# Last attention of a two-block model on one Trainium2 core: TensorE's scores issued for two steps at a time

## The chip, the cores and the metric

One core of one Trainium2 chip runs the whole program in one launch. The metric is the device time in microseconds (us), as the median of several runs. Engines are called TensorE (PE in the profile, PEld for its weight loads), VectorE (DVE), ScalarE (ACT), GpSimd (POOL) and SyncE (SP).

## The reference

The program computes two model blocks in a row on 512 tokens of width 1024. The first has a gated linear recurrence layer and a gated linear attention layer. The second has feed-forward layers, a stick-breaking attention and, last, an attention with three branches, whose mixer is what this document is about (16 query heads of 64, 4 key/value groups):

```python
s_c = einsum('btgrd,bcgd->bgrtc', q, k_c) * scale          # 31 compressed keys
p_c = softmax(where(valid_c, s_c, NEG)) * any(valid_c)
o_c = einsum('bgrtc,bcgd->btgrd', p_c, v_c)
o_s = _nsa_selected(q, sel_idx, k_s, v_s)                  # selected blocks
o_w = _nsa_window(q, k_w, v_w)                             # window of 512
o = gates[0] * o_c + gates[1] * o_s + gates[2] * o_w
return o.reshape(B, S, H * Dh) @ w_out
```

With 512 tokens there are 8 key blocks of 64 and 8 are selected, so the selected branch, like the window branch, is causal attention over all keys. One more feed-forward layer follows.

## The kernel before, in words

Each engine has one hand-written stream of instructions; the streams meet only by semaphores (`wait_ge` before an instruction, `then_inc` after it), and each engine takes its stream in order. Weights stream through a ring of four slots: SyncE loads a slot when GpSimd has split the one before it, GpSimd splits a weight into a high and a low part (L332, L334), and TensorE multiplies with three products per tile (L364 to L366).

The last attention (TensorE L1186 to L1281, ScalarE L1640 to L1677, VectorE L2260 to L2345, GpSimd L2419 to L2437) runs over 8 pairs of heads and six kinds of step per pair, 48 steps in all (`NSA_STEPS`, L574). `nsa_step(s)` gives pair s // 6, kind s % 6 and PSUM slot s % 2 * 2. Kinds 0 to 4 hold parts of the causal score matrix (`NSA_PARTS`, L572): kinds 0 and 2 have one part of 512 keys, kinds 1 and 3 have two parts (128 and 384 keys), kind 4 has two of 256. Kind 5 is the compressed branch. Each part exists for two heads. A step s passes through these operations:

- TensorE, scores (`nsa_scores`, L1186): products of queries and keys into the PSUM banks of slot s % 2, then the mask products (L1213, L1202). It waits for `probs_ready` of step s - 2 (L1194), which last read that slot.
- VectorE, maxima (`nsa_maxima`, L2260): the row maxima out of PSUM (L2279) and the bias; for kind 5 three passes (L2267, L2271, L2274).
- ScalarE, exponentials (`nsa_probs`, L1640): one activation per part and head (L1652), each with a read of the accumulated sum, and at the end `probs_ready`; one activation (L1645) for kind 5. From step 4 on it waits for the transposes of step s - 4.
- VectorE, coefficients (`nsa_coef`, L2292): gate over sum (L2311, L2313).
- GpSimd, scaling (`nsa_scale`, L2419): the probabilities times the coefficients (L2430; L2424 for kind 5).
- TensorE, transposes (`nsa_turn`, L1217): eight 128x128 transposes into PSUM banks 4 and 5 (L1231; L1229 for kind 5). They wait for the scaling of the step and for both copies of step s - 1.
- Copies of the transposed halves out of PSUM: bank 4 by VectorE (`nsa_low_half`, L2318), bank 5 by ScalarE (`nsa_high_half`, L1660).
- TensorE, values (`nsa_attend`, L1234): products with the values (L1253; L1245 for kind 5). They wait for both copies of step s.

After the last kind of a pair, ScalarE and VectorE read the pair's result (`nsa_mix_high` L1664, `nsa_mix_low` L2322). The output projection (`out_pe`) and the last feed-forward layer follow.

The order of each stream is written out by hand. In iteration `it` of its loop (L1275) TensorE issues the scores of step it + 2, the transposes of it - 1 and the values of it - 2. ScalarE (L1671) issues the copy of it - 1, the exponentials of it + 2, and, once a pair, the mix copy. VectorE (L2332) issues the maxima of it + 2, the coefficients of it + 1, the copy of it - 1, and, once a pair, the low mix; where step it + 2 is of kind 5 the copy and the coefficients come ahead of the maxima. In iterations 1 to 6 VectorE also carries the rotation of the last query tile (L2228, L2233, L2239, L2241).

Of the kernel before, what the change touches and what calls it, by code (L numbers as in the profile page):

```python
# [104 lines left out]
def build(nc, x_in, consts_in, gates_in, weights, out):  # L105
    ctx = ExitStack()
    with ctx:
# [72 lines left out]
        for name, slots, cols in STREAM:  # L180
            first[name] = n0
            n0 += slots
        slots_of = {name: slots for name, slots, _ in STREAM}
        cols_of = {name: cols for name, _, cols in STREAM}

        def used(name, n):
# [207 lines left out]
        def out_pe(pe, name, x_hi, x_lo, lows, free, banks=(4, 5, 6, 7)):  # L394

            def low_ready(k):
                return pe.wait_ge(sem["mix_low"], lows + k + 1)

            pe.wait_ge(sem["w_ready"], ready(name, 1))
            product(ps[:, banks[0], :], 0, DT, x_hi, x_lo, low_ready, last_k=DT - 1)  # L400
            pe.wait_ge(sem["w_ready"], ready(name, 2))
            product(ps[:, banks[1], :], 1, DT, x_hi, x_lo, last_k=3)
            product(ps[:, banks[0], :], 0, DT, x_hi, x_lo, low_ready, first_k=DT - 1)
            product(ps[:, banks[1], :], 1, DT, x_hi, x_lo, first_k=3)
            for m in range(2, DT):
                if m >= RING:
                    pe.wait_ge(sem[free[0]], free[1] + m - RING + 1)
                pe.wait_ge(sem["w_ready"], ready(name, m + 1))
                product(ps[:, banks[m % RING], :], m, DT, x_hi, x_lo)
# [153 lines left out]
        def pr_of(s, e):  # L563

            return prt[:, 1, e, :] if s == 0 else (root, acc)[e] if s == 1 else pr[:, s % 4, e, :]
# [8 lines left out]
        NSA_STEPS = SB_PAIRS * NSA_KINDS  # L574

        def nsa_step(s):

            return s // NSA_KINDS, s % NSA_KINDS, s % 2 * 2
# [51 lines left out]
        def _(pe):  # L630
# [520 lines left out]
            def q_norms(m):  # L1151
                pe.wait_ge(sem["q_copied"], m + 1)
                if m == 4:
                    pe.wait_ge(sem["norms_read"], 1)
                for t in range(TT):
                    mm = nc.tensor.matmul(ps[:, 7, t * 16 + 2 * m:t * 16 + 2 * m + 2], sq_q[:, m % 2, t * P:(t + 1) * P],
                                          con("halves")[:, 0:P:64], start=True, stop=True)
                mm.then_inc(sem["norms_mm"], 1)
# [27 lines left out]
            def nsa_scores(s):  # L1186

                p, kind, slot = nsa_step(s)
                if kind == 0:
                    pe.wait_ge(sem["q_rotated"], p + 1)  # L1190
                if s == 0:
                    pe.wait_ge(sem["q_shifted"], 6)
                if s >= 2:
                    pe.wait_ge(sem["probs_ready"], s - 1)  # L1194
                if kind == NSA_KINDS - 1:
                    for t in range(TT):
                        for e in range(2):
                            rows = slice(64 * e, 64 * e + 64)
                            nc.tensor.matmul(ps[:, slot + e, t * N_CMP:(t + 1) * N_CMP], q_r[rows, p, t * P:(t + 1) * P],
                                             k_c3[rows, p // 2, :], start=(t == 0), stop=False, skip_group_check=True)  # L1200
                    for e in range(2):
                        mm = nc.tensor.matmul(ps[:, slot + e, 0:TT * N_CMP], ident_1, neg_c_1, start=False, stop=True,  # L1202
                                              skip_group_check=True)
                else:
                    for i, (br, t, at) in enumerate(NSA_PARTS[kind]):
                        for e in range(2):
                            rows = slice(64 * e, 64 * e + 64)
                            nc.tensor.matmul(ps[:, slot + e, at:at + (t + 1) * P], q_r[rows, p, t * P:(t + 1) * P],
                                             k_sw[rows, p // 2 + 4 * br, 0:(t + 1) * P], start=(i == 0), stop=False,
                                             skip_group_check=True)  # L1210
                    for br, t, at in NSA_PARTS[kind]:
                        for e in range(2):
                            mm = nc.tensor.matmul(ps[:, slot + e, at + t * P:at + (t + 1) * P], ident_1, causal_1,  # L1213
                                                  start=False, stop=True, skip_group_check=True)
                mm.then_inc(sem["z2_done"], 1)

            def nsa_turn(s):  # L1217

                p, kind, _ = nsa_step(s)
                pe.wait_ge(sem["scaled"], s + 1)  # L1220
                if s == 0:
                    pe.wait_ge(sem["q_shifted"], 7)
                if s > 0:
                    pe.wait_ge(sem["low_half"], s)
                    pe.wait_ge(sem["high_half"], s)
                for e in range(2):
                    for t in range(TT):
                        if kind == NSA_KINDS - 1:
                            mm = nc.tensor.transpose(ps[0:N_CMP, 4 + e, t * P:(t + 1) * P], pr_c[:, e, t, :], ident)  # L1229
                        else:  # L1230
                            mm = nc.tensor.transpose(ps[:, 4 + e, t * P:(t + 1) * P], pr_of(s, e)[:, t * P:(t + 1) * P], ident)  # L1231
                mm.then_inc(sem["turned"], 1)

            def nsa_attend(s):  # L1234

                p, kind, _ = nsa_step(s)
                pe.wait_ge(sem["low_half"], s + 1)
                pe.wait_ge(sem["high_half"], s + 1)
                if kind == 0 and p == 1:
                    pe.wait_ge(sem["norms_read"], 2)  # L1240
                if kind == 0 and p >= 2:
                    pe.wait_ge(sem["mix_low"], 2 * DT + p - 1)
                if kind == NSA_KINDS - 1:
                    for e in range(2):
                        mm = nc.tensor.matmul(ps[64 * e:64 * e + 64, 6 + p % 2, :], v_c3[0:N_CMP, p // 2, :],  # L1245
                                              prt[0:N_CMP, s % 2, e, :], start=False, stop=True, skip_group_check=True)
                    mm.then_inc(sem["attended"], 1)
                    return
                first_mm = kind == 0
                for br, t, at in NSA_PARTS[kind]:  # L1250
                    for t2 in range(t + 1):
                        for e in range(2):
                            nc.tensor.matmul(ps[64 * e:64 * e + 64, 6 + p % 2, t * P:(t + 1) * P],  # L1253
                                             v_sw4[:, t2, p // 2 + 4 * br, :],
                                             prt[:, s % 2, e, at + t2 * P:at + (t2 + 1) * P],
                                             start=first_mm, stop=False, skip_group_check=True)
                        first_mm = False
# [14 lines left out]
            q_norms(DT - 2)  # L1272
            nsa_scores(2)
            q_norms(DT - 1)
            for it in range(1, NSA_STEPS + 2):  # L1275
                if it + 2 < NSA_STEPS:
                    nsa_scores(it + 2)
                if it - 1 < NSA_STEPS:
                    nsa_turn(it - 1)
                if 0 <= it - 2:  # L1280
                    nsa_attend(it - 2)  # L1281
            out_pe(pe, "nsa_out", mix2_hi, mix2_lo, 2 * DT, ("res_done", RES["nsa_out"]))
            ffn_pe("ffn2", 1, 3)

# [1075 lines left out]
        def _(pool):  # L2360
# [23 lines left out]
            for j in range(1, 2 * RING):  # L2384
                split_slot(pool, "odd_out", j // RING, j % RING)
            split_first(pool, "ffn1_in_0_0")
            split_pool(pool, *(name for name, _, _ in ffn_stream("ffn1", 0)[1:]), "sb_qk", "sb_v", "sb_late",
                       "sb_out", *(name for name, _, _ in ffn_stream("ffn2", 0)), "kv_c", "kv_kv")
            for n in range(7):
                split_slot(pool, "cmp_w1", n // RING, n % RING)  # L2390
# [214 lines left out]
```

## Time and profile before

| | us |
|---|---|
| median of 3 runs | 2743.24 (2742.39 to 2743.55) |
| the profiled execution | 2743.05 |
| its span in the trace | 2741.2 |
| TensorE busy | 2701.0 (99%) |
| GpSimd busy | 1629.6 (59%) |
| VectorE busy | 1321.7 (48%) |
| ScalarE busy | 711.8 (26%) |

The span is the time between the first and the last instruction of the trace; the profiled execution's own time is 1.8 us longer. Busy shares are averages over all stages. Busy times of TensorE are modelled at their ends, so start-to-start times are safer than durations. In a line of the timeline the columns are: start, time from the first start to the last end, engine, line, operation, what is written and read, and how many instructions of the kind are merged.

### The profile page before, as it was taken

The numbers are of one execution on the slowest core, as the hardware profiler recorded it, in microseconds if no ns is written. First come the engines' busy times: TensorE is split into PE (matmuls) and PEld (weight loads), VectorE is DVE, ScalarE is ACT, GpSimd is POOL, SyncE is SP. The second block draws the span as 40 slices with busy tenths as digits, with TensorE's granted clock in tenths as the row PEclk, the third lists the DMA queues.
The fourth block names the chain that finished last, engine by engine and source line by source line (L and its number), as shares of the span: only waits on it lengthen the run. The fifth ranks groups of instructions, "written<-read, shape, count | busy, mean of one in ns | idle before, by whom it ended". The sixth has DMA issues, their size and how long they took to land.

```text
span 2741.2 us, 35951 instructions
## 1 busy us (share of the span) xinstructions
PE 2701.0 (99%) x13142; PEld 2166.8 (79%) x13142; DVE 1321.7 (48%) x1601; ACT 711.8 (26%) x1235; POOL 1629.6 (59%) x947
## 2 busy tenths in 40 slices
PE   9999999999999999999999999999999999999999
PEld 6777777867888888867888888788888766888887
DVE  7878824574532461176440433642244777543242
ACT  4433423343200110284210113310011477211010
POOL 5566755514665666603665666566666799566565
PEclk9999999999999999999999999999999999999999
DMA  4322322202332323301332333433232100233232
GB/s 180 101 93 94 90 92 85 84 24 71 96 118 77 96 96 92 93 9 47 92 109 82 100 100 92 125 98 115 77 107 85 55 1 2 85 99 116 77 97 87
DMA packets 62028, 235.58 MB, mean 86 GB/s; under 512 B 6880, under 2 KB 7008, under 8 KB 61792
## 3 DMA queue, kind: packets, MB, share of 16 engines
q1 hardware_dynamic: 61920, 234.14, 27.0%
q8 instruction: 68, 1.11, 0.2%
q14 instruction: 40, 0.33, 0.0%
HBM read 232.02 MB, written 2.10 MB: 85 GB/s over the span
## 4 chain that ended last, share of the span: by engine, by line
PE 81%; DVE 6%; POOL 4%; PEld 3%; ACT 2%; issue 2%; DVEq 1%; PEldq 0%; DMA 0%; POOLq 0%; ACTq 0%; SPq 0%
PE ps L364 23%; PE ps L366 23%; PE ps L365 23%; POOL arena L2430 3%; PE ps L388 1%; PE ps L383 1%; PE ps L382 1%; PE ps L1038 1%; PEld ps L708 1%; PEld ps L709 1%; PEld ps L710 1%; PE ps L1022 1%; PE ps L660 1%; DVE arena L2279 0%; POOL w_lo L334 0%
## 5 line engine op out<-in xcount | busy, mean ns | idle before, releaser
L334 POOL TENSOR_TENSOR w_lo<-ring,w_hi 128x1024 fp32r<-128x1024 f32 (+2 forms) x382 | 992.6, 2598 | 55.1 <-issue 0.2
L332 POOL CAST w_hi<-ring 128x1024 fp32r<-128x1024 f32 (+2 forms) x382 | 436.6, 1143 | 907.1 <-PE ps L366 723.6
L364 PE MATMUL ps<-hi,w_hi 128*128 128x512 f32 x2064 | 810.2, 393 | 5.6 <-POOL w_lo L334 2.9
L366 PE MATMUL ps<-hi,w_lo 128*128 128x512 f32 x2064 | 804.0, 390 | 0.0
L365 PE MATMUL ps<-lo,w_hi 128*128 128x512 f32 x2064 | 803.9, 389 | 0.0
L364 PEld LDWEIGHTS ps<-hi,w_hi 128*128 128x128 f32 x2064 | 388.0, 188 | 92.1 <-POOL w_lo L334 4.8
L365 PEld LDWEIGHTS ps<-lo,w_hi 128*128 128x128 f32 x2064 | 387.9, 188 | 82.3 <-issue 2.6
L366 PEld LDWEIGHTS ps<-hi,w_lo 128*128 128x128 f32 x2064 | 387.9, 188 | 81.2
L364 PE MATMUL ps<-hid_hi,w_hi 128*128 128x512 f32 x704 | 274.4, 390 | 0.0
L365 PE MATMUL ps<-hid_lo,w_hi 128*128 128x512 f32 x704 | 273.9, 389 | 0.0
L366 PE MATMUL ps<-hid_hi,w_lo 128*128 128x512 f32 x704 | 273.9, 389 | 0.0
L2033 DVE TENSOR_TENSOR hid_lo<-arena,hid_hi 128x512 f32 (+1 forms) x88 | 222.2, 2525 | 80.2 <-ACT hid_hi L1505 80.2
L1503 ACT ACTIVATE ps<-ps 128x512 f32<-128x512 f32 x88 | 51.2, 582 | 629.4 <-DVE ps L2025 629.4
L2049 DVE SCALAR_TENSOR_TENSOR res<-ps,res 128x512 f32<-128x512 f32 x64 | 44.3, 691 | 343.8 <-PE ps L366 343.8
L2030 DVE TENSOR_TENSOR arena<-arena,ps 128x512 f32<-128x512 f32 x88 | 60.5, 687 | 275.5 <-PE ps L366 275.0
L1505 ACT ACTIVATE hid_hi<-arena 128x512 f32 (+1 forms) x88 | 55.7, 633 | 410.7 <-DVE arena L2030 410.7
L364 PEld LDWEIGHTS ps<-hid_hi,w_hi 128*128 128x128 f32 x704 | 132.2, 188 | 28.6 <-POOL w_lo L334 1.3
L366 PEld LDWEIGHTS ps<-hid_hi,w_lo 128*128 128x128 f32 x704 | 132.2, 188 | 27.6
L365 PEld LDWEIGHTS ps<-hid_lo,w_hi 128*128 128x128 f32 x704 | 132.2, 188 | 27.2
L2430 POOL TENSOR_SCALAR arena<-arena 128x512 f32<-128x512 f32 (+3 forms) x124 | 133.2, 1099 | 16.9 <-DVE arena L2313 16.7
L246 DVE SCALAR_TENSOR_TENSOR lo<-res,consts,hi 128x512 fp32r<-128x512 f32 x64 | 117.2, 1839 | 32.3 <-ACT hi L240 31.7
L2025 DVE TENSOR_TENSOR ps<-ps,rinv 128x512 f32<-128x512 f32 x88 | 61.5, 699 | 117.8 <-PE ps L366 107.7
(363 smaller groups left out, 3320.4 us busy)
## 6 DMA issues: line engine op xcount, KB each, us to landing
ring<-in_ffn_in SPq DMA_DIRECT2D x176, 512.0 KB, 3.6
ring<-in_even_in SPq DMA_DIRECT2D x48, 512.0 KB, 4.6
ring<-in_ffn_out SPq DMA_DIRECT2D x32, 768.0 KB, 4.3
ring<-in_ffn_out SPq DMA_DIRECT2D x32, 640.0 KB, 3.9
ring<-in_even_out SPq DMA_DIRECT2D x16, 512.0 KB, 3.6
ring<-in_sb_qk SPq DMA_DIRECT2D x12, 512.0 KB, 3.6
ring<-in_odd_v SPq DMA_DIRECT2D x8, 512.0 KB, 3.6
ring<-in_odd_r SPq DMA_DIRECT2D x8, 512.0 KB, 3.6
```

What stands on the lines that cost most here:

```text
L246: nc.vector.scalar_tensor_tensor(lo[:, t, :], res[:, t, :], con("g_" + f)[:, t:t + 1], hi[:, t, :].bitcast(F32), ALU.mult, ALU.subtract).t ...
L332: nc.gpsimd.tensor_copy(high[:, j % 2, 0:cols], ring[:, j, 0:cols])
L334: nc.gpsimd.tensor_tensor(low[:, j % 2, 0:cols], ring[:, j, 0:cols], high[:, j % 2, 0:cols].bitcast(F32), ALU.subtract).then_inc(sem["w_re ...
L364: nc.tensor.matmul(bank, w_hi[:, j % 2, w], x_hi[:, k, :], start=(k == 0), stop=False)
L365: nc.tensor.matmul(bank, w_hi[:, j % 2, w], x_lo[:, k, :], start=False, stop=False)
L366: mm = nc.tensor.matmul(bank, w_lo[:, j % 2, w], x_hi[:, k, :], start=False, stop=(k == kt - 1))
L1503: nc.scalar.activation(gate, gate, ACT.Silu).then_inc(sem["silu_done"], 1)
L1505: nc.scalar.activation(hid_hi[:, 2 * i + j, :], wide[:, j, :], ACT.Copy)\
L2025: V.tensor_tensor(gate, gate, rinv[:, :], ALU.mult).then_inc(sem["gate_scaled"], 1)
L2030: V.tensor_tensor(wide[:, j, :], wide[:, j, :], up, ALU.mult).then_inc(sem["hidden_wide"], 1)
L2033: V.tensor_tensor(hid_lo[:, 2 * i + j, :], wide[:, j, :], hid_hi[:, 2 * i + j, :].bitcast(F32), ALU.subtract)\
L2430: op = G.tensor_scalar(part, part, coef[:, s % 4, i, e:e + 1], None, ALU.mult)
```

## The change

TensorE's loop advances by two steps. It issues the scores of steps it + 2 and it + 3 together, and then the transposes of it - 1, the values of it - 2, the transposes of it and the values of it - 1. The set of instructions, their operands and their waits stay as they are; the streams of the other engines are not touched.

```diff
-            for it in range(1, NSA_STEPS + 2):
-                if it + 2 < NSA_STEPS:
-                    nsa_scores(it + 2)
-                if it - 1 < NSA_STEPS:
-                    nsa_turn(it - 1)
-                if 0 <= it - 2:
-                    nsa_attend(it - 2)
+            for it in range(1, NSA_STEPS + 2, 2):
+                for s in (it + 2, it + 3):
+                    if s < NSA_STEPS:
+                        nsa_scores(s)
+                for s in (it - 1, it):
+                    if s < NSA_STEPS:
+                        nsa_turn(s)
+                    if 0 <= s - 1 < NSA_STEPS:
+                        nsa_attend(s - 1)
             out_pe(pe, "nsa_out", mix2_hi, mix2_lo, 2 * DT, ("res_done", RES["nsa_out"]))
```

## Rows read from the trace of the kernel before

**Rows 1.** The page's first part: busy time of each engine.

```profile
PE 2701.0 (99%) x13142; PEld 2166.8 (79%) x13142; DVE 1321.7 (48%) x1601; ACT 711.8 (26%) x1235; POOL 1629.6 (59%) x947
```

**Rows 2.** Busy time by stage: length; PE, PEld, DVE, ACT, POOL; clock, DMA.

```profile
2178.74:2209.97 31.23, 29.89 (x307) 21.08 (x307) 26.95 (x65) 22.46 (x64) 28.34 (x28) 1.00 0.01 2
...
2249.62:2269.45 19.83, 19.56 (x198) 13.68 (x199) 14.43 (x37) 14.51 (x42) 17.63 (x17) 1.00 0.01 2
...
2309.12:2322.02 12.90, 12.90 (x132) 9.15 (x133) 8.94 (x23) 9.97 (x31) 10.73 (x10) 1.00 0.01 3
2322.02:2328.38 6.36, 4.19 (x51) 3.38 (x49) 4.12 (x11) 3.02 (x8) 6.36 (x8) 1.00 0.00 0
```

**Rows 3.** Timeline of PE, 2249 to 2270 us.

```profile
2249.62 1.06 PE L1231 MATMUL ps<-consts,arena 128*128 128x128 f32 x8 [0.28 <-POOL arena L2424]
2250.62 1.09 PE L1253 MATMUL ps<-arena 128*64 128x128 f32 x16
2251.64 1.13 PE L1208 MATMUL ps<-arena 64*128 64x512 f32 x4
...
2258.10 1.13 PE L1208 MATMUL ps<-arena 64*128 64x256 f32 x8
...
2259.40 1.04 PE L1231 MATMUL ps<-consts,arena 128*128 128x128 f32 x8
...
2262.53 1.04 PE L1231 MATMUL ps<-consts,arena 128*128 128x128 f32 x8
...
2264.53 1.13 PE L1208 MATMUL ps<-arena 64*128 64x512 f32 x4
...
2265.71 1.04 PE L1231 MATMUL ps<-consts,arena 128*128 128x128 f32 x8
```

**Rows 4.** Waits of the five pairs from 2209.97 to 2309.12: total us, times, longest.

```profile
PE ps L1231 <- POOL arena L2424: 1.9, 6, 0.5
```

**Rows 5.** Timeline of PE at the stage's start, 2174 to 2182 us.

```profile
2176.66 1.14 PE L1208 MATMUL ps<-arena 64*128 64x256 f32 x8
...
2181.99 1.05 PE L1231 MATMUL ps<-consts,arena 128*128 128x128 f32 x8
```

**Rows 6.** Timeline of ACT, 2176 to 2190 us.

```profile
2176.40 0.19 ACT L1652 ACTIVATION_READ_ACCUMULATOR arena<-ps,arena 128x1 f32 x1
...
2189.43 0.19 ACT L1652 ACTIVATION_READ_ACCUMULATOR arena<-ps,arena 128x1 f32 x1
```

**Rows 7.** Timeline of ACT, 2250 to 2270 us.

```profile
2250.73 0.60 ACT L1660 ACTIVATE arena<-ps 128x512 f32<-128x512 f32 x1 [0.98 <-PE ps L1231]
2251.22 0.45 ACT L1652 ACTIVATE arena<-ps,arena 128x128 f32<-128x128 f32 x1
...
2261.16 0.56 ACT L1652 ACTIVATE arena<-ps,arena 128x256 f32<-128x256 f32 x1
...
2263.25 0.21 ACT L1652 ACTIVATION_READ_ACCUMULATOR arena<-ps,arena 128x1 f32 x1
2263.56 0.60 ACT L1664 ACTIVATE mix_hi<-ps 128x512 fp32r<-128x512 f32 x1
...
2267.95 0.78 ACT L1652 ACTIVATE arena<-ps,arena 128x512 f32<-128x512 f32 x1 [0.55 <-DVE arena L2284]
...
2269.38 0.20 ACT L1652 ACTIVATION_READ_ACCUMULATOR arena<-ps,arena 128x1 f32 x1
```

**Rows 8.** Timeline of DVE, 2263 to 2267 us.

```profile
2263.61 0.69 DVE L2318 COPY arena<-ps 128x512 f32<-128x512 f32 x1 [1.24 <-PE ps L1231]
2264.22 0.17 DVE L2311 RECIPROCAL arena<-arena 128x4 f32<-128x4 f32 x1
...
2266.47 1.21 DVE L2279 TENSOR_REDUCE arena<-ps 128x2 f32<-128x1024 f32 x1
```

**Rows 9.** Scalings on POOL by shape, 2209.97 to 2309.12 us.

```profile
L2430 POOL TENSOR_SCALAR arena<-arena 128x256 f32<-128x256 f32 x20 | 18.2, 935 | 0.0
```

**Rows 10.** Busy time in 5 us of an earlier stage, columns as in rows 2.

```profile
85.00:90.00 5.00, 2.30 (x7) 0.76 (x5) 4.78 (x4) 3.40 (x6) 4.11 (x3) 1.00 0.77 296
```

## The prediction

> **What bounds the kernel now.** I read four views, in this order. The page's busy times [rows 1] put TensorE at 99% of the span: what holds TensorE's queue lengthens the kernel, and other work is free while it is hidden. The busy times by stage [rows 2] then show what one pair of heads costs in the attention: 19.83 us, in which TensorE is busy 19.56 and GpSimd 17.63. ScalarE has 14.51 and VectorE 14.43, so both idle a quarter of the time; by totals neither is a bound. The timeline of TensorE [rows 3] shows how the 19.83 us are filled: transposes to values take 1.00 us from start to start (2249.62 to 2250.62), values to scores 1.02 (to 2251.64), scores with masks to transposes 1.30 for two-part kinds (2258.10 to 2259.40) and 1.18 for one-part kinds (2264.53 to 2265.71). It hardly waits. The one repeated wait, of the transposes for GpSimd, is 1.9 us over five pairs [rows 4]. So the order of before keeps TensorE full with a small margin, and the question is how much time the new order leaves the other engines between a result and its use.
>
> **The change, part by part.** No instruction is added or removed. Call S, T and A the scores, transposes and values on TensorE, C the ScalarE copy of the transposed half, E the exponentials. The old order is S(5) T(2) A(1) S(6) T(3) A(2). The new one is S(5) S(6) T(2) A(1) T(3) A(2). One thing moves: the score blocks of even steps go ahead of a transpose and a value block. Nothing is moved past DMA issues: the ring's next loads hang on GpSimd's splits, and GpSimd has none between its scalings.
>
> *The moved block's wait.* S(s) waits for E(s-2), whose PSUM slot it overwrites; for S(6) this is E(4). Both orders have two rounds of TensorE's work, some 6.6 us, between the starts of S(4) and S(6), and both ask ScalarE for C(1) and E(4) in that time. But in the old order T(0) lies ahead of S(4), so C(0) and most of E(3) run beside it. In the new order T(0) comes behind S(4), C(0) can't begin before T(0), and ScalarE's stream is in strict order: C(0), E(3), C(1), E(4). So a loop closes, for odd a: T(a-3), C(a-3), E(a), C(a-2), E(a+1), S(a+3), T(a-1). All four ScalarE jobs stand between one pair of score blocks and the next, while TensorE stands at S(a+3) with transposes queued behind it that could run. In the old order E(a+1) is followed by the same S(a+3), but C(a-2) follows T(a-2) closely, and the loop T(a-2), C(a-2), E(a+1), S(a+3), T(a) holds one C and one E in two rounds: it has room.
>
> *The loop's length.* T start to C start is 1.11 us (2249.62 to 2250.73) [rows 3, 7]. C start to E start is 0.49 (2250.73 to 2251.22), four-part exponentials last 2.30 (2261.16 to 2263.46), one-part ones with two heads 1.63 (2267.95 to 2269.58), and from the end of E to ScalarE's next instruction it is 0.10 (2263.46 to 2263.56) [rows 7]. From the end of E to the start of the scores that waited for it is 0.07: S(4) begins at 2176.66, when E(2) ends at 2176.59 [rows 5, 6]; this one wait shows the mechanism in the old order already. The fixed part is 1.11 + 0.49 + 0.10 + 0.49 + 0.07 = 2.26 us. The three groups of a pair then are:
>
> - Transposes of kind 4 to those of kind 0, exponentials of kinds 1 and 2: 2.26 + 2.30 + 1.63 + 1.30 = 7.49 us.
> - Transposes of kind 0 to kind 2, exponentials of kinds 3 and 4: 2.26 + 2.30 + 2.30 + 1.18 = 8.04 us.
> - Transposes of kind 2 to kind 4, exponentials of kind 5 and of kind 0 of the next pair. Here VectorE sets the pace, since for kind 5 it copies and makes coefficients before the maxima, and the maxima of the next step come behind (2263.61, 2264.22, 2266.47) [rows 8]. The old trace holds this chain whole: transposes at 2262.53, end of exponentials at 2269.58 [rows 3, 7], 7.05 us. Then 0.07 + 1.18 of scores: 8.30 us.
>
> A pair takes 23.83 us instead of 19.83, 4.00 more. TensorE's own work per pair stays at 19.4, so some 4.4 us of each pair is waiting.
>
> *Over the stage.* Before the loop nothing changes up to S(4) at 2176.66. T(0) follows at 2177.96. Five groups lead to T(10): 8.04, then the kind 5 group in its first form, with query rotation on VectorE (2181.99 to the end of exponentials at 2189.62 [rows 5, 6], 7.63, and 1.25: 8.88), then 7.49, 8.04 and 8.30. That is 40.75, T(10) at 2218.71 against 2209.97 [rows 2]: 8.7 more. Five pairs: 5 x 4.00 = 20.0. From T(40) to T(44): 7.49 + 8.04 = 15.53 against 12.90 [rows 2]: 2.6. From T(44) to T(46) no more scores wait, and GpSimd's scaling ends last: coefficients at 1.69 after the transposes (2262.53 to 2264.22) [rows 3, 8], some 0.5 to GpSimd's start, four parts of 0.935 [rows 9], 0.1: 6.0 against 6.36 [rows 2], 0.3 less. After T(46) the order is the old one. The sum is 8.7 + 20.0 + 2.6 - 0.3 = 31.0 us.
>
> *What I cost at nothing.* GpSimd's scalings have room: coefficients for kind 4 come 1.7 us after the transposes of kind 2, scaling ends near 5.9, and its transposes come at 8.3; if this cover went, each pair would pay what lies over 8.3. The second transposes of a group need both copies of the first, which end 1.8 us after the first began (2262.53 to 2264.30 [rows 3, 8]); TensorE gets there at 2.0. Were they late, 0.9 us would still be hidden, since the copy that they release stands behind exponentials until 4.0, and could start at 3.1. GpSimd's weight splits behind the stage start later with it and stay hidden behind products.
>
> *What the trace doesn't show.* Two score blocks in a row, and transposes right behind values, inside the stage. Neither is in the loop, which at S(a+3) starts from standstill. So the unknown is whether hand-overs keep their length under the new alignment. There are six in a loop of about 0.1 us beyond the work; at 0.05 each either way it is 0.3 a loop and 7 us over 23 loops. I take the measured values: 2743.05 + 31.0 = 2774.0 us. The profiled execution is 0.19 below the median of the runs, which changes nothing.
>
> *A rule beside the row.* S(4) began 0.07 us after the exponentials' end, though transposes were queued behind it [rows 5, 6]; the row shows the hold, not whether the next block could have passed. The Trainium skill, TensorE: Matmul & The Clock Gate, in Part 2 (what happens when you issue a matmul), says that TensorE pulls weight loads ahead but keeps matmuls in program order. By that rule the queue behind S waits in full and the sum stands; without it the first rival below would hold.
>
> **The rivals.**
>
> *The scores do not hold the queue.* If the exponentials are done before S(a+3) is reached, or the transposes run past it, only the gain is left: scores in hand ahead of the transposes that waited for GpSimd, 1.9 us over five pairs [rows 4] and about as much at the ends. 2743.05 - 4 = 2739, not slower. It decides if the loop is shorter than TensorE's 6.6 us per group. Against it: the loop is 7.5 at its shortest and made of measured pieces, and would have to lose 0.9 us. Chance 0.05.
>
> *A partial loss.* Pieces that overlap in the trace (an activation begins while the one before drains) could overlap more when the data is already there. With 0.5 us less per loop the loss is 31 - 11.5 = 19.5: 2762. Chance 0.07.
>
> *A further engine joins the loop.* If VectorE's maxima, which stand behind the copy of the first transposes, end after ScalarE is free (I have them 1.2 us early), or GpSimd's scaling does, each group adds up to 0.5 us: 31 + 11.5, 2785 us. Chance 0.07.
>
> *The clock falls with the waits.* TensorE would stand idle in each group. In 5 us with TensorE busy 2.30 us the granted clock stayed at 1.00, that is 2.4 GHz [rows 10], and the new stretch is busier, at 80%. At 1.2 GHz its 6.5 us a group would become 13: 5 us above the loop's 8, 23 times, 2889 us. The same page of the Trainium skill, Part 1 (the HAM clock gate), says that idleness brings the lower of the two rates; the row here shows none of it. Chance 0.02.
>
> **How the numbers follow.** The forecast case has 0.79 and by itself reaches from 2766 to 2782. Taking in the partial loss down to 2761 and half of the case above, to 2785, leaves less than 0.2 outside. A measurement of this kernel can tell 0.2%, 5.5 us, from no change. Faster by more than this would need more than the first rival gives: 0.02. Within: 0.04. Slower, the four other cases: 0.94.
>
> **What would show it.** In the changed profile, TensorE's scores should wait for ScalarE once in two steps, 1 to 2 us each; the wait should be on every second score block alone; a pair should take 23.8 us with groups of 7.5, 8.0 and 8.3; T(10) should start near 2218.7 and ScalarE should show no idle time between C and E in the two groups with two exponentials. GpSimd should idle some 6 us per pair. The stages before 2176 and after the attention should take what they take now. It is wrong if TensorE's wait lies at the transposes, if the pair stays below 21 us, or if the granted clock in the stage falls below 1.00.

## The result, and the profile after

| | before | after |
|---|---|---|
| median, us | 2742.39 (2741.17 to 2743.55, 5 runs) | 2790.47 (2789.30 to 2792.58, 5 runs) |
| span of the profiled execution, us | 2741.2 | 2788.7 |
| mean granted clock | 0.999 | 0.991 |

The ratio is 1.0175 (95% interval 1.0164 to 1.0187): the change makes the kernel 48 us slower. The forecast was slower by 31 us, 2774, with a range from 2761 to 2785. The direction is right; the size is not, and the time lies outside the range.

The page of the changed kernel: its first part, the clock row and the chain's second row.

```profile
PE 2724.6 (98%) x13142; PEld 2178.9 (78%) x13142; DVE 1355.6 (49%) x1601; ACT 709.0 (25%) x1235; POOL 1623.8 (58%) x947
...
PEclk9999999999999999999999999999999988999999
...
PE ps L364 23%; PE ps L365 23%; PE ps L366 23%; ACTq L1657 2%; PE ps L388 1%; PE ps L1208 1%; PE ps L382 1%; PE ps L383 1%; PE ps L1038 1%; ACT arena L1654 1%; PE ps L1231 1%; PEld ps L708 1%; PEld ps L709 1%; PEld ps L710 1%; PE ps L660 1%
```

Two things are new against [rows 1]. TensorE is busy 23.6 us longer though it executes the same 13142 instructions, and two slices of the clock row are 8. In the chain, the end of the exponentials (ACTq L1657, the drain that signals them; lines after the edit are two higher than before) stands where GpSimd's scaling (POOL arena L2430, 3%) stood.

Where the time lies can be read from three marks. From the start of the scores of step 4 to the transposes of step 46 it is 151.7 us before (2176.66 to 2328.38 [rows 2, 5]) and 201.2 after (2174.56 to 2375.78). From there to the end of the span it is 412.8 before and 412.9 after. The attention alone is 49.5 us longer; the stages ahead of it ended 2.1 us earlier in this execution.

One pair of heads in the changed kernel, TensorE's timeline, from the transposes of kind 4 to those of the next pair (the answer to [rows 3]):

```profile
2219.85 1.66 PE L1231 MATMUL ps<-consts,arena 128*128 128x128 f32 x8
2221.44 1.09 PE L1253 MATMUL ps<-arena 128*64 128x128 f32 x16
2222.46 1.06 PE L1229 MATMUL ps<-consts,arena 128*31 128x128 f32 x8
...
2224.48 1.14 PE L1208 MATMUL ps<-arena 64*128 64x128 f32 x8
...
2226.59 1.13 PE L1208 MATMUL ps<-arena 64*128 64x256 f32 x8 [0.65 <-ACTq L1657]
...
2227.90 1.04 PE L1231 MATMUL ps<-consts,arena 128*128 128x128 f32 x8
...
2231.92 1.08 PE L1199 MATMUL ps<-arena 64*128 64x31 f32 x16
...
2234.81 2.08 PE L1208 MATMUL ps<-arena 64*128 64x512 f32 x4 [1.59 <-ACTq L1657]
...
2237.01 1.61 PE L1231 MATMUL ps<-consts,arena 128*128 128x128 f32 x8
...
2241.62 1.14 PE L1208 MATMUL ps<-arena 64*128 64x128 f32 x8
...
2244.87 1.98 PE L1208 MATMUL ps<-arena 64*128 64x512 f32 x4 [1.77 <-ACTq L1657]
...
2246.97 1.75 PE L1231 MATMUL ps<-consts,arena 128*128 128x128 f32 x8
```

The second score block of each group, and no other, waits for ScalarE: 0.65, 1.59 and 1.77 us. That is the forecast loop. But behind the two long waits the work itself is slower: scores of a one-part kind take 2.08 and 1.98 us where they took 1.13 in [rows 3], transposes 1.61 and 1.75 where they took 1.04. Behind the short wait they take what they took. Not every long wait is followed by this: one of 1.59 us in the first 35 us of the stage is not.

```profile
2209.18 1.13 PE L1208 MATMUL ps<-arena 64*128 64x512 f32 x4 [1.59 <-ACTq L1657]
...
2210.37 1.04 PE L1231 MATMUL ps<-consts,arena 128*128 128x128 f32 x8
```

The groups of the pair above last 8.05, 9.11 and 9.96 us against 7.49, 8.04 and 8.30 forecast, the pair 27.12 against 23.83.

The busy times of that pair (columns as in [rows 2]) and the groups by line over five pairs, 2219.85 to 2355.77 (count, then busy us, mean ns, idle before):

```profile
2219.85:2246.97 27.12, 23.10 (x201) 15.39 (x199) 15.00 (x36) 14.16 (x40) 17.73 (x18) 0.88 0.01 2
```

```profile
L1208 PE MATMUL ps<-arena 64*128 64x384 f32 (+3 forms) x160 | 36.5, 568 | 20.1 <-ACTq L1657 20.1
L1231 PE MATMUL ps<-consts,arena 128*128 128x128 f32 x200 | 33.7, 324 | 0.0
L1253 PE MATMUL ps<-arena 128*64 128x128 f32 x400 | 27.4, 279 | 0.0
L1213 PE MATMUL ps<-masks 128*128 128x128 bf16 x82 | 10.3, 243 | 0.0
```

The granted clock is 0.88 over the pair, where it was 1.00: part of each pair runs at the lower level, 1.2 GHz instead of 2.4. By the busy row, TensorE works 23.10 us of the pair and stands 4.02, against 19.56 and 0.27 in [rows 2]: 3.54 us more of work and 3.75 more of standstill make the 7.29. The lines say where. In five pairs of the kernel before, by the same view of 2209.97 to 2309.12:

```profile
L1208 PE MATMUL ps<-arena 64*128 64x128 f32 (+3 forms) x160 | 28.4, 462 | 0.0
L1253 PE MATMUL ps<-arena 128*64 128x128 f32 x400 | 27.4, 279 | 0.0
L1231 PE MATMUL ps<-consts,arena 128*128 128x128 f32 x201 | 26.5, 274 | 1.9 <-POOL arena L2424 1.9
L1213 PE MATMUL ps<-masks 128*128 128x128 bf16 x80 | 8.8, 222 | 0.0
```

Waiting for the exponentials is 20.1 us in five pairs, 4.0 a pair, and the wait for GpSimd, 1.9 us in five pairs, is gone. Scores, transposes and masks are longer by 8.1 + 7.2 + 1.5 = 16.8 us, 3.4 a pair, while the values, which come when the clock is back, have not changed. That is a reading of two traces; the experiments test both halves.

### The profile page after: what moved, and what is told of

Same layout as the page of the kernel before. It is cut to its first block, busy times and chain, and to the rows that moved or that the text cites. A ratio compares the mean times of both kernels' runs of the same rounds, so it can differ in the third digit from the quotient of the medians.

```text
span 2788.7 us, 35951 instructions
## 1 busy us (share of the span) xinstructions
PE 2724.6 (98%) x13142; PEld 2178.9 (78%) x13142; DVE 1355.6 (49%) x1601; ACT 709.0 (25%) x1235; POOL 1623.8 (58%) x947
## 3 DMA queue, kind: packets, MB, share of 16 engines
q8 instruction: 68, 1.11, 0.2%
## 4 chain that ended last, share of the span: by engine, by line
PE 83%; DVE 5%; PEld 3%; ACT 3%; issue 2%; ACTq 2%; DVEq 1%; POOL 1%; PEldq 0%; POOLq 0%; DMA 0%; SPq 0%
PE ps L364 23%; PE ps L365 23%; PE ps L366 23%; ACTq L1657 2%; PE ps L388 1%; PE ps L1208 1%; PE ps L382 1%; PE ps L383 1%; PE ps L1038 1%; ACT arena L1654 1%; PE ps L1231 1%; PEld ps L708 1%; PEld ps L709 1%; PEld ps L710 1%; PE ps L660 1%
## 5 line engine op out<-in xcount | busy, mean ns | idle before, releaser
L246 DVE SCALAR_TENSOR_TENSOR lo<-res,consts,hi 128x512 fp32r<-128x512 f32 x64 | 144.9, 2273 | 32.3 <-ACT hi L240 31.7
```

What stands on the lines that cost most here:

```text
L246: nc.vector.scalar_tensor_tensor(lo[:, t, :], res[:, t, :], con("g_" + f)[:, t:t + 1], hi[:, t, :].bitcast(F32), ALU.mult, ALU.subtract).t ...
```

## The experiments

**The theory** had by now two parts. A: TensorE's second score block waits for a loop through ScalarE, which costs what the forecast says. B: the rest is the lower clock that the standstills bring. The rivals: the loop is longer than sized and the clock only accompanies it; the waits have another origin than the place of the transposes.

### TensorE kept at work while it waits

```diff
                 for s in (it + 2, it + 3):
+                    if s == it + 3 and 6 <= s < NSA_STEPS:
+                        pe.wait_ge(sem["high_half"], s - 4)
+                        for _ in range(4 if s % NSA_KINDS == 4 else 9):
+                            nc.tensor.matmul(ps[:, 5, 0:3 * P], ident_1, masks[:, 0:3 * P], start=True, stop=True)
                     if s < NSA_STEPS:
                         nsa_scores(s)
```

The added wait makes sure that ScalarE has copied bank 5 before the products overwrite it.

> The changed kernel with TensorE kept at work while it waits: ahead of each waiting score block it issues 9 dummy products of 384 columns (4 where the waiting step is of kind 4) into PSUM bank 5, which the next transposes overwrite. Theory (the loop through ScalarE costs 31 us as sized, and the 16 us above it are the lower clock that the waits bring): granted clock 1.00 in the stage, a pair near 23.8 us, 2772 to 2778 us. Rival (the loop itself is longer than sized, the clock only shows it): a pair stays near 27 us and the time within 3 us of 2790.

Measured: 2773.25 us (2772.48 to 2774.67), ratio 1.0106 (1.0089 to 1.0123). Busy times of one pair and of the stage, then TensorE's timeline of the pair:

```profile
2244.84:2268.84 24.00, 23.55 (x222) 15.66 (x221) 15.01 (x37) 14.16 (x40) 17.83 (x17) 1.00 0.01 1
2170.00:2380.00 210.00, 201.92 (x1814) 138.43 (x1813) 132.13 (x304) 116.79 (x327) 155.16 (x144) 1.00 0.03 9
```

```profile
2244.84 1.04 PE L1231 MATMUL ps<-consts,arena 128*128 128x128 f32 x8
...
2252.27 1.04 PE L1231 MATMUL ps<-consts,arena 128*128 128x128 f32 x8
...
2257.43 1.63 PE L1280 MATMUL ps<-masks 128*128 128x384 bf16 x9
2259.18 1.13 PE L1208 MATMUL ps<-arena 64*128 64x512 f32 x4
...
2260.37 1.04 PE L1231 MATMUL ps<-consts,arena 128*128 128x128 f32 x8
...
2265.72 1.63 PE L1280 MATMUL ps<-masks 128*128 128x384 bf16 x9
2267.66 1.13 PE L1208 MATMUL ps<-arena 64*128 64x512 f32 x4 [0.32 <-ACTq L1661]
...
2268.84 1.04 PE L1231 MATMUL ps<-consts,arena 128*128 128x128 f32 x8
```

Useless work makes the kernel faster than the changed one: it is 29.2 us above the kernel before on the same chip (2744.01), where the changed kernel is 48.1 above (2742.39). The clock stays at 1.00, scores take 1.13 us and transposes 1.04, and the groups last 7.43, 8.10 and 8.47 us, 24.00 in all, where the forecast said 7.49, 8.04, 8.30 and 23.83. Both parts of the theory hold: the loop costs what was worked out, and what lies above it is the clock, 27.12 - 24.00 = 3.1 us a pair. The filling itself doesn't set the 24.00: a kernel further down, with one product in place of nine, has 24.11 in a pair at full clock.

### The first transposes back ahead of the second scores

```diff
-                for s in (it + 2, it + 3):
-                    if s < NSA_STEPS:
-                        nsa_scores(s)
-                for s in (it - 1, it):
-                    if s < NSA_STEPS:
-                        nsa_turn(s)
-                    if 0 <= s - 1 < NSA_STEPS:
-                        nsa_attend(s - 1)
+                if it + 2 < NSA_STEPS:
+                    nsa_scores(it + 2)
+                if it - 1 < NSA_STEPS:
+                    nsa_turn(it - 1)
+                if it + 3 < NSA_STEPS:
+                    nsa_scores(it + 3)
+                if 0 <= it - 2 < NSA_STEPS:
+                    nsa_attend(it - 2)
+                if it < NSA_STEPS:
+                    nsa_turn(it)
+                if it - 1 < NSA_STEPS:
+                    nsa_attend(it - 1)
```

> TensorE's order is S(a) T(a-3) S(a+1) A(a-4) T(a-2) A(a-3): the first transposes go back ahead of the second scores, the values stay behind them. Theory (what costs is that T stands behind the second S, so that the ScalarE copy starts late): from T(a-4) to the end of the exponentials of a-1 it is 4.0 us, TensorE has 4.3 us of work before S(a+1), so no wait of more than 0.2 us, clock 1.00, 2739 to 2748 us. Rival (two score blocks close together are too early for the exponentials in any case): waits of 1 us or more stay at every second score block, over 2765 us.

Measured: 2745.94 us (2743.02 to 2747.93), ratio 1.0007 (0.9997 to 1.0016). One pair:

```profile
2253.25:2273.52 20.27, 19.96 (x199) 13.78 (x199) 15.07 (x37) 14.28 (x42) 17.71 (x17) 1.00 0.01 2
```

20.27 us a pair, and no score block of the pairs waits for the exponentials (one did near the start of the stage, 0.80 us at 2186.62). Putting the transposes back is enough: it is their place behind the second scores that costs, not that the scores of two steps lie close. Compared with the kernel before there is no gain.

### The pairs shifted by one step

```diff
-            for it in range(1, NSA_STEPS + 2, 2):
+            nsa_scores(3)
+            nsa_turn(0)
+            for it in range(2, NSA_STEPS + 2, 2):
```

> The same order with the pairs shifted by one step: scores of even and odd steps (4,5), (6,7) together, so that the exponentials of a loop are of kinds (0,1), (2,3) and (4,5). Theory: by the same sum the loops are 7.5, 7.3 and 7.5 us, 22.3 us a pair of heads, each wait about 0.9 us. If the clock falls only with waits of 1.6 us and more, as the trace of the changed kernel shows it (it stayed at a wait of 0.65 and of 0.99 us), the clock stays at 1.00 and the time is 2760 to 2767 us. If it falls with any standstill, 2775 us or more. If the loop is not ScalarE's, the time does not follow this sum and stays near 2790.

Measured: 2766.15 us (2763.86 to 2767.43), ratio 1.0083 (1.0066 to 1.0100). Two of the waiting score blocks of one pair, and the pair:

```profile
2243.69 1.14 PE L1208 MATMUL ps<-arena 64*128 64x128 f32 x8 [0.76 <-ACTq L1659]
...
2251.12 1.08 PE L1199 MATMUL ps<-arena 64*128 64x31 f32 x16 [0.64 <-ACTq L1659]
```

```profile
2236.24:2258.39 22.15, 20.00 (x198) 13.76 (x198) 14.84 (x37) 14.05 (x40) 17.84 (x18) 1.00 0.01 1
```

A pair lasts 22.15 us where the sum by the same rows gave 22.3. The three waits are 0.64 to 0.76 us, where 0.9 was expected, and the clock is at 1.00 from 2220 us on. Score blocks issued two and two thus cost 22 us or 48 us, by which kinds of exponentials meet in a loop and by whether the standstills lower the clock. Near the start of the stage they did in this kernel too: the clock was at 0.94 in the first 30 us, with standstills up to 2.73 us, and a standstill of 1.29 us at 2203.83 was followed by transposes of 1.92 us.

### ScalarE's exponentials ahead of its copies

```diff
             for it in range(1, NSA_STEPS + 3):
-                if it - 1 < NSA_STEPS:
+                if it % 2 and it + 2 < NSA_STEPS:
+                    nsa_probs(it + 2)
+                if it % 2 and it - 1 < NSA_STEPS:
                     nsa_high_half(it - 1)
-                if it + 2 < NSA_STEPS:
+                if it % 2 == 0 and it + 2 < NSA_STEPS:
                     nsa_probs(it + 2)
+                if it % 2 == 0 and it - 1 < NSA_STEPS:
+                    nsa_high_half(it - 1)
```

Written for odd and even iterations apart, the edit puts the exponentials first in both.

> TensorE's order as in the change; ScalarE issues the exponentials of it + 2 ahead of the copy of it - 1. Theory (ScalarE's strict order closes the loop): E(a) leaves the loop, which becomes T(a-3), C(a-3), maxima(a+1), E(a+1), S(a+3), T(a-1), some 6.9 us in two of the three groups; in the group with kind 5, where VectorE sets the pace, 8.3 us and the lower clock stay. 2752 to 2762 us. Rival (ScalarE's order is not what holds): no change against the changed kernel, 2787 us or more.

Measured: 2800.75 us (2798.46 to 2801.88), ratio 1.0209 (1.0192 to 1.0226). A miss: the exchange was expected to give time back, and the kernel is 10 us slower than the changed one (9 us by the runs of before beside each). TensorE's and ScalarE's timeline around one group:

```profile
2242.30 1.04 PE L1231 MATMUL ps<-consts,arena 128*128 128x128 f32 x8
...
2245.74 0.41 ACT L1647 ACTIVATE arena<-arena 128x248 f32<-128x248 f32 x1 [4.63 <-DVE arena L2280]
2246.06 0.58 ACT L1662 ACTIVATE arena<-ps 128x512 f32<-128x512 f32 x1
...
2246.78 1.46 PE L1231 MATMUL ps<-consts,arena 128*128 128x128 f32 x8 [2.41 <-ACT arena L1662]
```

The score blocks of the pairs no longer wait; the second transposes of each group do, 2.41 us here and 1.46 and 1.55 us in the other two, for a copy that now stands behind E(a). I had taken E(a) as ready before the first transposes. But S(a) and S(a+1) now run together right ahead of them, and VectorE's maxima of a come late: in the group shown, where VectorE copies first for kind 5, E(a) begins 3.44 us after the first transposes (2242.30 to 2245.74); in the next it begins 0.48 us after them (2252.95 to 2253.43), but lasts 2.3. The pair from 2242.30 on takes 26.89 us at a clock of 0.94, against 27.12, and the longest 28.5. By its number the run falls to the rival, 2787 us or more; but the wait has moved from the scores to the transposes, so ScalarE's order does decide which block waits. The expectation failed in what it left out, the wait of the second transposes for the copy of the first.

### A third of the filling, and a ninth

```diff
-                        for _ in range(4 if s % NSA_KINDS == 4 else 9):
+                        for _ in range(0 if s % NSA_KINDS == 4 else 3):
```

> As the filled kernel, with 3 dummy products ahead of the waiting score blocks of kinds 0 and 2 (some 0.54 us) and none ahead of kind 4: standstills of 0.65 us a pair in one group and of about 1.1 to 1.2 us in the other two are left, between the 0.76 us at which the kernel with the other pairing kept its clock and the 1.59 us at which the changed kernel lost it. If a fill of a third is enough: clock 1.00 from pair to pair, 2771 to 2777 us. If any standstill over 1 us is enough to lower the clock: it falls as in the changed kernel and the time is 2785 us or more.

Measured: 2775.39 us (2773.48 to 2777.29), ratio 1.0119 (1.0101 to 1.0137). Then one product instead of three:

> As the filled kernel, with one dummy product ahead of the waiting score blocks of kinds 0 and 2 and none ahead of kind 4: standstills of some 1.5 us in two of three groups. The kernel with three products kept its clock in most pairs with standstills of 1.1 to 1.3 us and lost it in a few; the changed kernel lost it in every pair at 1.6 to 1.8 us. If the length of the standstill decides between these, 1.5 us lies on the losing side: 2783 to 2791 us. If any work in between is enough: 2772 to 2778 us.

Measured: 2778.87 us (2774.12 to 2782.08), ratio 1.0128 (1.0111 to 1.0145). Its profile, of the execution of 2774.12 us, shows standstills as long as one of those that cost the changed kernel its clock, and no loss behind them; the one loss of this trace is near the start of the stage, behind 1.52 us at 2184.53:

```profile
2258.21 1.13 PE L1208 MATMUL ps<-arena 64*128 64x512 f32 x4 [1.44 <-ACTq L1661]
...
2266.69 1.13 PE L1208 MATMUL ps<-arena 64*128 64x512 f32 x4 [1.62 <-ACTq L1661]
```

A pair of this kernel, at full clock and with hardly any filling, lasts 24.11 us:

```profile
2251.29:2275.40 24.11, 20.31 (x203) 13.95 (x201) 15.03 (x36) 14.17 (x40) 17.85 (x18) 1.00 0.01 1
```

The kernel with three products had, in its profile, one group at the lower clock (not a few, as the expectation has it) and its neighbours not:

```profile
2242.01 1.13 PE L1208 MATMUL ps<-arena 64*128 64x512 f32 x4 [1.29 <-ACTq L1661]
...
2257.64 1.62 PE L1208 MATMUL ps<-arena 64*128 64x512 f32 x4 [1.11 <-ACTq L1661]
2259.38 1.92 PE L1231 MATMUL ps<-consts,arena 128*128 128x128 f32 x8
```

So 0.3 us of work in each long wait gives back most of what the clock had cost (34.0 us above the kernel before, where it was 48.1 without and 29.2 with nine), but not in every execution: the four runs with one product took 2774.1, 2777.8, 2780.0 and 2782.1 us at mean clocks of 0.999, 0.998, 0.996 and 0.995. The length of the single standstill does not decide it: 1.11 us lost the clock once and 1.62 us kept it, and in the changed kernel 1.59 us kept it at 2209.18 and lost it at 2234.81. My expectation, that 1.5 us lies on the losing side, fell between its two cases. What decides is left open.

### The two copies of the transposed halves

In the first of three, ScalarE copies 128 of 512 columns from step 6 on, on top of the filled kernel (here with 5 products ahead of kind 0, 9 ahead of kind 2 and none ahead of kind 4):

```diff
-                nc.scalar.activation(prt[0:rows, s % 2, 1, :], ps[0:rows, 5, :], ACT.Copy).then_inc(sem["high_half"], 1)
+                n = T if s < 6 else P
+                nc.scalar.activation(prt[0:rows, s % 2, 1, 0:n], ps[0:rows, 5, 0:n], ACT.Copy).then_inc(sem["high_half"], 1)
```

> The filled kernel, and from step 6 on ScalarE copies 128 of the 512 columns of its transposed half (the values of these steps are left wrong). That takes about 0.32 us off each copy. Theory (both copies of a group stand in the loop): each loop of the two groups without kind 5 is 0.64 us shorter, the group with kind 5, which VectorE paces, stays: 8 pairs x 2 x 0.64 = 9 to 10 us less than the filled kernel, 2762 to 2766 us. Rival (ScalarE's copies are beside the loop): 2773 us as before the cut.

Measured: 2764.38 us (2763.00 to 2765.37), ratio 1.0078 (1.0060 to 1.0096). Transposes of kinds 4, 0, 2 and 4 again:

```profile
2240.02 1.04 PE L1231 MATMUL ps<-consts,arena 128*128 128x128 f32 x8
...
2246.91 1.04 PE L1231 MATMUL ps<-consts,arena 128*128 128x128 f32 x8
...
2254.37 1.04 PE L1231 MATMUL ps<-consts,arena 128*128 128x128 f32 x8
...
2262.85 1.04 PE L1231 MATMUL ps<-consts,arena 128*128 128x128 f32 x8
```

The groups are 6.89, 7.46 and 8.48 us against 7.43, 8.10 and 8.47 of the filled kernel: 0.54 and 0.64 us off the two that ScalarE paces, nothing off the one with kind 5. The same cut in the kernel before:

> The kernel before with the same short copy on ScalarE from step 6 on (the values of these steps are left wrong). Theory: in the old order ScalarE's loop has room, so the cut gives nothing, within 3 us of before. Rival (ScalarE's copy already paces the old order): 10 us or more less.

Measured: 2742.80 us (2740.56 to 2745.61), ratio 0.9997 (0.9987 to 1.0007). Nothing, as expected: in the old order the copy has room. And VectorE's copy cut in the filled kernel:

```diff
-                V.tensor_copy(prt[0:rows, s % 2, 0, :], ps[0:rows, 4, :]).then_inc(sem["low_half"], 1)
+                n = T if s < 6 else P
+                V.tensor_copy(prt[0:rows, s % 2, 0, 0:n], ps[0:rows, 4, 0:n]).then_inc(sem["low_half"], 1)
```

> The filled kernel, and from step 6 on VectorE copies 128 of the 512 columns of its transposed half (the values of these steps are left wrong; 6 instead of 9 dummy products ahead of kind 2). Theory: VectorE's copy stands in the loop only in the group with kind 5, so this group alone gets shorter, by some 0.4 us (8.47 to about 8.1), and the two others stay at 7.4 and 8.1 us; 2770 us. Rival (VectorE paces the other groups as well): all three get shorter by 0.3 us or more.

Measured, one run: 2772.89 us. The transposes of kinds 4, 0, 2 and 4 start at 2244.63, 2252.06, 2260.16 and 2268.23: groups of 7.43, 8.10 and 8.07 us. Only the group with kind 5 got shorter, by 0.40 us; this is read from the one trace, since a single run can't tell the 3 us forecast. So each engine's share of the loop lies where the forecast put it.

### Another filling

```diff
-                        for _ in range(4 if s % NSA_KINDS == 4 else 9):
-                            nc.tensor.matmul(ps[:, 5, 0:3 * P], ident_1, masks[:, 0:3 * P], start=True, stop=True)
+                        for _ in range(6 if s % NSA_KINDS == 4 else 12):
+                            nc.tensor.transpose(ps[:, 5, 0:P], ident, ident)
```

> The filled kernel with another filling: 12 transposes of a 128x128 float32 tile (6 ahead of kind 4) in place of the 9 (4) products of 384 columns, for about the same 1.6 us of TensorE time. If the clock takes transposes for work like products: granted clock 1.00 in the stage, 2772 to 2777 us. If it does not count transposes, as the Trainium skill has it in TensorE: Matmul & The Clock Gate, Part 4 (PE-mode transpose): the clock falls as in the changed kernel, 2785 to 2793 us, though TensorE never stands still.

Measured: 2772.88 us (2770.07 to 2774.60), ratio 1.0110 (1.0093 to 1.0126). The stage:

```profile
2170.00:2380.00 210.00, 199.82 (x1870) 146.75 (x1869) 131.72 (x301) 114.86 (x321) 153.67 (x142) 1.00 0.03 9
```

Filled with transposes, the kernel keeps its clock as it does with products. The rule of the Trainium skill that the expectation names (TensorE: Matmul & The Clock Gate, Part 4) is not borne out here, 1.00 and 2772.88 us against the 2785 or more that it would give, and the measurement decides, for float32 transposes of 128x128 issued among products. Two limits: the profile lists these transposes as MATMUL and doesn't show whether they run in the mode that the page means, and the run doesn't say that they count in full, since one product in each long wait was nearly enough too.

## Why the prediction was wrong in size and right in kind

- **What bounds the kernel.** Right: TensorE's queue, with a small margin, and the other engines' lead as the thing that changes.
- **The moved block's wait.** Right: only S(a+3) waits, for the exponentials' end, and the transposes queue behind it. Moving them back ahead of it removes nearly all of the loss (20.27 us a pair, 2745.94 us).
- **The loop's length.** Right: 24.00 us a pair at full clock (24.11 with hardly any filling) against 23.83. The largest miss of a group is 0.17 us, in the one with kind 5. The cuts of the copies and the other pairing (22.15 against 22.3) confirm the pieces.
- **Over the stage.** 31.0 us were summed; with the clock held, the medians differ by 29.2 (2773.25 against 2744.01), interval 24 to 34 us. That is close in part by luck: the sum has T(42) to T(44) at 8.04 us, as if S(48) held the queue, but the steps end at 47, and the filled kernel's trace has 5.15 (2348.28 to 2353.43). The 2.9 us too many there hide some 1.5 that the loops and the last waits for GpSimd took beyond the sum.
- **The missing term.** The sum had no term for the clock, and this is the step that failed. Against the filled kernel it measured 3.1 us a pair (27.12 against 24.00). Over the whole, the changed kernel is 48.1 us above the kernel before, the filled one 29.2 us above the runs of before beside it: 18.9 us between them. The rival "The clock falls with the waits" was the right mechanism with a chance of 0.02. Its price was wrong too: 2889 us, as if the lower level held throughout, where the mean of the stage was 0.89.
- **The row that misled.** [rows 10] was read as "TensorE may be idle half the time and keep 2.4 GHz". But the stretch ends where its standstill of 2.70 us ends, at 89.92. The next 5 us of the same trace are at 0.66, the only stretch of 5 us in the kernel before whose clock is below 1.00, and the products behind the standstill take 0.63 us where they took 0.39 before it (83.17):

```profile
90.00:95.00 5.00, 5.00 (x15) 4.00 (x16) 1.70 (x3) 4.88 (x6) 3.70 (x2) 0.66 0.35 109
```

```profile
89.92 0.58 PE L364 MATMUL ps<-hi,w_hi 128*128 128x512 f32 x1 [2.70 <-POOL w_lo L334]
90.29 0.63 PE L365 MATMUL ps<-lo,w_hi 128*128 128x512 f32 x1
```

So the trace of before held the warning: what a standstill does to the clock shows in the rows behind it. The changed kernel repeats standstills of 1.6 to 1.8 us in two groups of three, and lost clock behind the first long one already (1.68 us at 2182.77, then transposes of 1.91 us). The rule in the Trainium skill that I had cited beside the row, that idleness brings the lower rate (TensorE: Matmul & The Clock Gate, Part 1), is what this trace agrees with: 0.88 with the standstills, 1.00 with them filled.

- **What would show it wrong.** The prediction named a clock below 1.00 in the stage, and that is what the profile shows. The range ended at 2785, since it left out the case that joined the forecast mechanism with a lower clock; they are not alternatives, the first causes the second, as the filled kernel shows.

## What to carry to other kernels

When an order of issue is written by hand, follow each block that is moved ahead to what it waits for, and ask whether the producer's own stream begins with something that is now queued behind the block: if so a loop closes, and its length is the sum of whole jobs, not the engine's busy share (ScalarE was idle a quarter of the time and still paced two groups of three). Price standstills of TensorE twice: the wait itself, and the work behind it at the lower clock; here the second was 3.1 us a pair beside 4.2. To see from a trace whether a standstill costs clock, read the granted clock behind it, not beside it. Where a wait of more than a microsecond couldn't be avoided, even one throwaway product in it gave back a good part (48 us of loss became 34), and nine gave back what the clock had cost (29).

## What the runs showed of the hardware

- Repeated standstills of 1.59 to 1.78 us in a busy stretch lowered the granted clock to 0.88 on the mean of a pair; in the pair shown, scores at the lower level took 1.98 to 2.08 us instead of 1.13 and transposes 1.61 to 1.75 instead of 1.04. The clock was back within about two blocks.
- In the kernel before, a single standstill of 2.70 us was followed by a clock of 0.66 over 5 us.
- The effect is not a function of the length of one standstill: 1.11 us was followed by the lower level once, 1.62 us was not, 1.59 us was and was not, and the same kernel took 2774.1 to 2782.1 us from run to run, in the order of its mean clock. Its four runs spread over 8.0 us, those of the kernel with nine products over 2.2.
- Float32 transposes as filling kept the clock at 1.00 as bf16 products did (2772.88 and 2773.25 us).
